# Branch merging in the list of weight blocks, gate blocks of the third mixer in the second's heads, token rows by DMA, query norm in the output norm

## The reference

```
u = rmsnorm(h) * valid                          # h: 16 learned tokens, 512 tokens
a_*, b_*, c_*, gate_logits = split(u @ w_in)    # 3 x 1024 columns are gate logits
y_a = hgrn2(...)          # 4 heads, decays per channel
y_b = gated_deltanet(...) # 4 heads: q, k, v = silu(conv(.)); q, k = l2norm; q *= 128**-0.5
                          # log decay and beta: one value per token and head
y_c = gla(...)            # 4 heads of 64 channels, decays per channel
# each mixer: y = rmsnorm(o, w) * silu(g) per head
proj   = einsum('blne,ned->blnd', [y_a, y_b, y_c], w_branch)     # 3 x (512 -> 1024)
merged = sum(sigmoid(gate_logits) * proj, over the 3 branches)
h = h + merged @ w_out
h = h + hierarchical_moe(rmsnorm(h))            # top 1 of 4 groups, top 2 of its 8 experts
return rmsnorm(h)                               # of the 512 tokens
```

## Time and profile before

| | |
|---|---|
| median of three runs | 1236.06 us |
| the runs | 1233.9 to 1239.37 us |
| the profiled execution | 1235.11 us |
| its span | 1233.3 us |
| granted clock of TensorE, mean | 0.944 |
| PE busy | 1083.6 us (88%) |
| PEld busy | 652.1 us (53%) |
| DVE busy | 466.2 us (38%) |
| ACT busy | 284.3 us (23%) |
| POOL busy | 57.1 us (5%) |

### The profile page before, as it was taken

The page is one execution under the profiler, slowest core; times in us unless marked ns, Lnnn a source line. Parts: engine busy times, 40 slices in busy tenths (PEclk is TensorE's granted clock), DMA queues, the critical chain, the costliest instruction groups (busy, mean ns, idle before and its releaser), DMA issues.

```text
span 1233.3 us, 15605 instructions
## 1 busy us (share of the span) xinstructions
PE 1083.6 (88%) x6346; PEld 652.1 (53%) x6346; DVE 466.2 (38%) x950; ACT 284.3 (23%) x540; POOL 57.1 (5%) x66
## 2 busy tenths in 40 slices
PE   6999999989989999899899898998974888788690
PEld 5665666665756757564645544443553444444350
DVE  3536354456373553734324321332335111111124
ACT  2524334133241332413203216000000111011012
POOL 0000000000000000000000000000001111111110
PEclk9999999999999999999999999998975998898995
DMA  9221222211111112112220105406331999999965
GB/s 282 63 69 52 68 52 69 52 52 35 38 49 35 52 36 52 35 35 56 64 53 26 52 26 210 131 0 236 127 120 35 413 415 408 401 396 402 417 231 219
DMA packets 113886, 171.53 MB, mean 139 GB/s; under 512 B 8726, under 2 KB 90855, under 8 KB 105507
## 3 DMA queue, kind: packets, MB, share of 16 engines
q1 hardware_dynamic: 100818, 131.19, 31.2%
q10 hardware_dynamic: 8080, 31.00, 6.6%
q0 software_dynamic: 4928, 8.50, 2.0%
HBM read 166.47 MB, written 12.58 MB: 145 GB/s over the span
## 4 chain that ended last, share of the span: by engine, by line
PE 73%; DMA 11%; DVE 9%; ACT 3%; issue 2%; POOL 1%; SPq 0%; POOLq 0%; DVEq 0%; ACTq 0%
PE ps L669 22%; DMA gates<-normed_tokens,gates 10%; PE ps L666 7%; PE ps L667 7%; PE ps L1583 7%; PE ps L1609 5%; PE ps L1910 4%; DVE arena L1197 3%; PE ps L1903 2%; PE ps L714 2%; PE ps L1897 2%; PE ps L723 2%; PE ps L693 1%; POOL expert_results L1871 1%; DVE yT L2189 1%
## 5 line engine op out<-in xcount | busy, mean ns | idle before, releaser
L669 PE MATMUL ps<-arena 128*128 128x512 f32 x672 | 317.5, 609 | 1.6 <-ACT arena L1162 1.6
L669 PEld LDWEIGHTS ps<-arena 128*128 128x128 f32 x672 | 120.9, 192 | 119.5 <-issue 114.3
L666 PE MATMUL ps<-arena 128*128 128x264 f32 x416 | 129.4, 393 | 10.0 <-DVE arena L1197 8.7
L667 PE MATMUL ps<-arena 128*128 128x264 f32 x416 | 128.1, 390 | 0.0
L1903 PE MATMUL ps<-arena,gates 128*64 128x256 f32 x1024 | 118.3, 385 | 1.5 <-DVE gates L2017 1.5
L1197 DVE TENSOR_TENSOR arena<-arena 128x512 f32<-128x512 f32 (+6 forms) x186 | 86.7, 511 | 83.9 <-ACT arena L1024 67.1
L1903 PEld LDWEIGHTS ps<-arena,gates 128*64 128x64 f32 x1024 | 74.7, 140 | 55.8 <-issue 23.5
L666 PEld LDWEIGHTS ps<-arena 128*128 128x128 f32 x416 | 75.7, 193 | 24.7 <-issue 14.9
L667 PEld LDWEIGHTS ps<-arena 128*128 128x128 f32 x416 | 80.1, 193 | 13.9
L1583 PE MATMUL ps<-yT,arena 128*128 128x512 f32 x192 | 84.4, 603 | 2.8 <-DVEq L93 2.8
L1910 PE MATMUL ps<-arena,gates 128*64 128x512 f32 x256 | 75.3, 719 | 0.0
(11 more groups left out here) (307 smaller groups left out, 1193.3 us busy)
## 6 DMA issues: line engine op xcount, KB each, us to landing
arena<-in_w_in SPq DMA_DIRECT2D x68, 512.0 KB, 3.9
arena<-in_expert_w_gate SPq DMA_DIRECT2D x32, 1024.0 KB, 10.0
arena<-in_expert_w_up SPq DMA_DIRECT2D x32, 1024.0 KB, 13.0
arena<-in_expert_w_down ACTq DMA_DIRECT2D x28, 1024.0 KB, 12.1
arena<-in_w_branch SPq DMA_DIRECT2D x8, 768.0 KB, 4.8
arena<-in_w_out SPq DMA_DIRECT2D x1, 4096.0 KB, 12.9
arena<-in_expert_w_down SPq DMA_DIRECT2D x4, 1024.0 KB, 13.3
arena<-expert_results SPq DMA_DIRECT2D x8, 512.0 KB, 6.8
```

The costliest lines, as they stand in the source:

```text
L666: t.matmul(dst[:, 0:HALF], wt, uT[:, k, 0:HALF], start=(k == 0), stop=(k == KD - 1))
L667: mm = t.matmul(dst[:, HALF:], wt, uT[:, k, HALF:], start=(k == 0), stop=(k == KD - 1))
L669: mm = t.matmul(dst, wt, uT[:, k, META:], start=(k == 0), stop=(k == KD - 1))
```

## The change

1. **The merge joins the list.** Its 12 blocks stand behind the segments of c: ("m", "ab", n), n = 0 to 7, is the a and b part of output column n (8 steps), three of them in the first round of c, five in the second; ("m", "c", n), n = 0 to 3, is the c part of two columns (8 steps), all at the end of the list, two of its blocks for each group of four columns. Their weights take slots of the same ring. On DVE merged(n) multiplies both parts with their gates and adds, within the levels of c; merged_last(n) does the c part. The loop L1574 to L1583 goes.
2. **Gate blocks.** t0 to t3 of the two rounds of c move to the four heads of b, two to each, which now hold four. Fills in b change: six steps before the sum for k and four before the products of k and k, then fill(4) twice around the transposes, where it was two, and fill(2) instead of fill(1) ahead of a level's second product.
3. **Gates in the mixers.** The sigmoid is made of Abs, Exp and Ln on ACT (gate_begin), a minimum and a difference on DVE (gate_part), and Exp on ACT (gate_end), inside the mixers.
4. **Token rows by transfer.** In the third head of a PE transposes log decay sums and beta into 20 rows of 256, which go to HBM once. In each head of b two DMAs on POOL's queue bring them back, broadcast over the 128 partitions (128 x 5 x 128 each). The POOL copies and the products G and B go; DVE's pass that takes the difference reads SBUF.
5. **Query norm.** q is no longer normalised. The sum over o squared gets a second matmul over q squared, with the small constants in its bias, so that the factor of q falls out of the output norm. The sum for q, its logarithm, its inverse root and the product go.
6. **Gates g.** In b and c the raw g is copied to SBUF early (gc), and v's blocks wait for that copy instead of the product.

```diff
         A_SEGS = ["f", "q", "g", "v", "t0", "t1"]
...
-        C_SEGS = ["k", "q", "g0", "g1", "v0", "v1", "t0", "t1", "t2", "t3"]
-        blocks = ([("a", s, r) for r in range(A_R) for s in A_SEGS] + [("b", s, r) for r in range(B_R) for s in B_SEGS] +
-                  [("c", s, r) for r in range(C_R) for s in C_SEGS])
+        C_SEGS = ["k", "q", "g0", "g1", "v0", "v1"]
+        M_AT = [3, 5]
+        blocks = [("a", s, r) for r in range(A_R) for s in A_SEGS]
+        for r in range(B_R):
+            blocks += [("b", s, r) for s in B_SEGS] + [("c", f"t{2 * (r % 2) + n}", r // 2) for n in range(2)]
+        n_first = 0
+        for r in range(C_R):
+            blocks += [("c", s, r) for s in C_SEGS] + [("m", "ab", n) for n in range(n_first, n_first + M_AT[r])]
+            n_first += M_AT[r]
+        blocks += [("m", "c", n) for n in range(4)]
...
         def mixers_gpsimd(g):
-            g.wait_ge(*dve0.after("gkm"))
+            g.wait_ge(*dve0.after("gbrow"))
+            g.dma_start(rows_dram, token_rows).then_inc(sem("rows_sent"), 16)
+            g.wait_ge(sem("rows_sent"), 16)
+            rv = rows_dram.rearrange("(t h) (k p) -> k h t p", h=B_R, k=2)
             for r in range(B_R):
                 g.wait_ge(*(b_pe.after(f"o.{r - 1}") if r else a_dve.after(f"y.{A_R - 1}")))
-                g.tensor_copy(t5(b_la), head_col(q_la, r)).then_inc(*b_pool.did(f"la.{r}"))
-                g.tensor_copy(t5(b_be), head_col(q_beta, r)).then_inc(*b_pool.did(f"be.{r}"))
+                g.dma_start(t5(b_gr), rv[0, r].unsqueeze(0).broadcast_to([P, NTP, P])).then_inc(sem("decay_rows"), 16)
+                g.dma_start(t5(b_br), rv[1, r].unsqueeze(0).broadcast_to([P, NTP, P])).then_inc(sem("beta_rows"), 16)
...
+                    if seg[0] == "t":
+                        t.wait_ge(*gate_read("b", int(seg[1]) % 2, 2 * r + int(seg[1]) // 2))
+                    elif seg == "k":
+                        if r:
+                            t.wait_ge(*m_dve.after(f"ab{2 * ((M_AT[0] - 1) // 2)}"))
+                        else:
+                            t.wait_ge(*gate_read(*channel_gates(B_R - 1, 0)))
+                    else:
+                        t.wait_ge(*c_dve.after({"q": "k", "g0": "f", "g1": "q", "v0": "gc_0", "v1": "gc_1"}[seg] + f".{r}"))
+                elif seg == "ab":
+                    if r == 0:
+                        t.wait_ge(*b_dve.after(f"y.{B_R - 1}"))
+                    if r in (0, 1, M_AT[0], M_AT[0] + 1):
+                        t.wait_ge(*c_act.after(f"vc_{1 - r % 2}.{int(r >= M_AT[0])}"))
+                    else:
+                        t.wait_ge(*m_dve.after(f"ab{r - 2}"))
+                elif r == 0:
+                    t.wait_ge(*m_dve.after(f"ab{KD - 1}"))
                 else:
-                    t.wait_ge(*c_dve.after({"q": "k", "g0": "f", "g1": "q", "v0": "g_0", "v1": "g_1"}[seg] + f".{r}"))
+                    t.wait_ge(*c_dve.after(f"y_{CH - 1}.{C_R - 1}"))
...
+                if stage == "m":
+                    if seg == "ab":
+                        b, wt, rhs = (k // 4, r), ring[:, n % RING, k, :], yT[:, k, :]
+                        first, last = k % 4 == 0, k % 4 == 3
+                    else:
+                        b, wt, rhs = (2, r // 2 * 4 + k % 4), ring[:, n % RING, k, :], yT[:, KD + r % 2 * 2 + k // 4, :]
+                        first, last = r % 2 == 0 and k < 4, r % 2 == 1 and k >= 4
+                    mm = t.matmul(merge_bank[b], wt, rhs, start=first, stop=last)
+                    if k == KD - 1:
+                        mm.then_inc(sem("block_done"), 1)
...
-                sums(bank(4), b_d[:, 0:SEQ]).then_inc(*b_pe.did(f"ss.{r}"))
+                t.matmul(bank(4), ones[:, :], b_d[:, 0:SEQ], start=True, stop=False)
+                t.matmul(bank(4), ones[:, :], b_kb[:, 0:SEQ], start=False, stop=True).then_inc(*b_pe.did(f"ss.{r}"))
...
                 through("b", "q", r)
-                t.wait_ge(*b_pool.after(f"la.{r}"))
-                t.wait_ge(*(b_dve.after(f"y1.{r - 1}") if r else a_dve.after(f"y1.{A_R - 1}")))
-                for c in range(NTP):
-                    mm = t.matmul(pair(6)[:, c * P:(c + 1) * P], b_la[:, c * P:(c + 1) * P], inc, start=True, stop=True)
-                mm.then_inc(*b_pe.did(f"G.{r}"))
-                fill(3)
+                fill(6)
                 t.wait_ge(*b_act.after(f"kk.{r}"))
                 t.wait_ge(*(b_act.after(f"ri.{r - 1}") if r else a_act.after(f"ri.{A_R - 1}")))
                 sums(pair(4)[:, 0:512], b_kb[:, 0:512])
                 sums(pair(4)[:, 512:], b_kb[:, 512:]).then_inc(*b_pe.did(f"ssk.{r}"))
-                fill(3)
-                t.wait_ge(*b_pool.after(f"be.{r}"))
-                t.wait_ge(*b_dve.after(f"dif.{r}"))
-                t.wait_ge(*b_act.after(f"eg.{r}"))
-                for c in range(NTP):
-                    mm = t.matmul(pair(6)[:, c * P:(c + 1) * P], b_be[:, c * P:(c + 1) * P], ident, start=True, stop=True)
-                mm.then_inc(*b_pe.did(f"B.{r}"))
                 through("b", "v", r)
+                fill(4)
                 t.wait_ge(*b_dve.after(f"kb.{r}"))
                 products(pair(4), b_kf, b_kb).then_inc(*b_pe.did(f"KK.{r}"))
-                fill(4)
-                t.wait_ge(*b_act.after(f"qq.{r}"))
-                sums(pair(6)[:, 0:512], b_vn[:, 0:512])
-                sums(pair(6)[:, 512:], b_vn[:, 512:]).then_inc(*b_pe.did(f"ssq.{r}"))
                 through("b", "g", r)
                 t.wait_ge(*b_dve.after(f"U.{r}"))
                 turn(pair(4), b_u).then_inc(*b_pe.did(f"N.{r}"))
-                t.wait_ge(*b_act.after(f"lnq.{r}"))
+                t.wait_ge(*(b_dve.after(f"y1.{r - 1}") if r else a_dve.after(f"y1.{A_R - 1}")))
                 turn(pair(6), b_kf).then_inc(*b_pe.did(f"kT.{r}"))
...
+                fill(4)
+                t.wait_ge(*b_dve.after(f"qr.{r}"))
                 t.wait_ge(*b_act.after(f"N.{r}"))
                 gram(bank(4), b_kf[:, P:], b_qf[:, P:]).then_inc(*b_pe.did(f"QK.{r}"))
-                fill(2)
...
-                    fill(1)
+                    fill(2)
...
-                    fill(1)
+                    fill(2)
...
-            assert not left
             c_out(C_R - 1)
+            fill(4)
             c_sum(C_R - 1)
+            fill(len(left))
         def mixers_scalar(a):
-            def gate(stage, n, r):
+            def gate_begin(stage, n, r):
+                g, row = gate_no(stage, n, r), gates[:, gate_row(stage, n, r), :]
                 a.wait_ge(*block_done(stage, f"t{n}", r))
-                a.activation(gates[:, gate_blocks.index((stage, f"t{n}", r)), :], real(n % 2), ACT.Copy).then_inc(sem("gate_read"), 1)
+                a.activation(row, real(n % 2), ACT.Abs).then_inc(sem("gate_size"), 1)
+                a.wait_ge(sem("gate_size"), g)
+                a.activation(row, row, ACT.Exp, scale=-1.0).then_inc(sem("gate_small"), 1)
+                a.wait_ge(sem("gate_small"), g)
+                a.activation(row, row, ACT.Ln, bias=one_c).then_inc(sem("gate_soft"), 1)
+            def gate_end(stage, n, r):
+                row = gates[:, gate_row(stage, n, r), :]
+                a.wait_ge(*gate_read(stage, n, r))
+                a.activation(row, row, ACT.Exp).then_inc(sem("gate_made"), 1)
...
                     tt(c_dve, f"y_{s}.{r}", yT[:, 8 + 2 * r + s, :], c_zz[s], c_g[s])
+            def gate_part(stage, n, r):
+                row = gates[:, gate_row(stage, n, r), :]
+                v.wait_ge(sem("gate_soft"), gate_no(stage, n, r))
+                v.scalar_tensor_tensor(row, real(n % 2), 0.0, row, ALU.min, ALU.subtract).then_inc(sem("gate_read"), 1)
+            def merged(n):
+                two = gates[:, n:2 * KD:KD, :]
+                if n == 0:
+                    v.wait_ge(sem("gate_made"), NB * KD)
+                v.wait_ge(*block_done("m", "ab", n))
+                v.tensor_tensor(two, ps[:, 2 * (n % 2) * 512:2 * (n % 2) * 512 + 1024].rearrange("p (b t) -> p b t", b=2), two, ALU.mult
+                                ).then_inc(*m_dve.did(f"ab{n}"))
+                v.wait_ge(*m_dve.after(f"ab{n}"))
+                tt(m_dve, f"s{n}", two[:, 0, :], two[:, 0, :], two[:, 1, :], ALU.add)
+            def merged_last(n):
+                row, sum_ = gates[:, 2 * KD + n, :], gates[:, n, :]
+                v.wait_ge(*block_done("m", "c", n // 4 * 2 + 1))
+                tt(m_dve, f"c{n}", row, merge_bank[2, n], row)
+                v.wait_ge(*m_dve.after(f"c{n}"))
+                tt(m_dve, f"h{n}", sum_, sum_, row, ALU.add)
...
+                        v.tensor_copy(c_g[l], real(1 - l)).then_inc(*c_dve.did(f"gc_{l}.{r}"))
+                    if l in (2, 3):
+                        s = l - 2
...
                             pick(c_dve, f"P{l - 1}_{s}.{r}", c_pm[s], l - 1, gram_bank(s))
+                    if l >= 4:
+                        merged(l - 4 + (M_AT[0] if r else 0))
                 for s in range(CH):
```

(12 more changed lines are left out.)

235 lines of the change are left out of this document (116 added, 119 removed).

## The result

| | before | changed |
|---|---|---|
| median | 1235.05 us (4 runs, 1233.9 to 1239.37) | 1216.62 us (4 runs, 1213.94 to 1217.12) |
| profiled execution, its span | 1235.11, 1233.3 us | 1213.94, 1212.1 us |
| ratio | | 0.9836, 95% interval 0.9816 to 0.9856 |

The change saves 18 us between the medians, 20 us by the ratio, 1.6%. Forecast were 1212 and a range of 1200 to 1226.

The account below looks back on a forecast made before the run. PE's work and waits were taken to bound the kernel. Terms +0.3 + 39.5 - 8.5 - 5 - 49.5 = -23.2 us on the profiled 1235.1 gave 1212 us, with an 8-in-10 range of 1200 to 1226.

Parts of the forecast that it names:

- What bounds it: Whole kernel to 751 us: time falls only by work taken from PE or waits filled; gain near 50 us, not 84.
- First mixer, +0.3: First mixer: extra gate passes cost nothing as PE never waits; transposed token rows add 0.3 us.
- Second mixer, heads 2 to 4, +9.7 each: Second mixer, per head: 11.3 us more PE work, 3.2 of waits gone, 1.6 of new wait at v's convolution.
- Second mixer, first head, +10.4: Second mixer's first head: the usual 9.7 us plus about 0.7 for token rows landing 5.5 us after issue.
- Third mixer, -8.5 and -5: Third mixer's two heads: v-block waits of 4.4 us go, first head has one block less; wait before level 5 stays.
- The end, -49.5: Last head's sums to output projection: 92.8 us becomes 43.3, with 27.5 of c blocks and 6.0 of idle PE.
- The remark that I left alone: Output projection: its first 32 products take 30.4 us where 27.5 would do; noted, with no term in the sum.
- More is hidden: Rival: v's convolution not late and clock stays up in the third mixer, giving 1202 us; chance 0.13.
- Less is hidden: Rival: second mixer keeps its waits and adds the new one, 12.9 us a head, giving 1225; chance 0.16.
- Rows late: Rival: second-mixer token rows land late; each us over 11.5 costs 4, slower than before from 17.5; chance 0.05.
- the port that the prediction named beside this rival: Token-row transfers from GpSimd: stall while VectorE holds the shared SBUF port, adding below 1 us, no change of the sum.
- Hold-up among merges: Rival: DVE merge passes awaiting PE blocks delay level work; eight at 3 us each leave no gain, near 1236; chance 0.06.

Follow-up runs that it names:

- the repeat: The changed kernel itself, unedited, run again on the same chip as three of the edits: 1218.56 us, ratio to before 0.9872.
- the split kernel: Changed kernel with the output projection started after four of the eight merged columns are summed, the rest after the last sum: 1209.89 us.
- the kernel with four edits: Changed kernel with first head's rows sent early, third-mixer state passes and gate copy behind the picks, and projection split: 1191.58 us, ratio 0.964.
- the one with five edits: Changed kernel with first rows early, states and gate copy behind picks, projection split, and v's convolution first: 1182.53 us, ratio 0.9579.

## Why the prediction was right, and where it was off

**What bounds it.** Right. PE's work and waits explain each stretch, and the gain is work removed and waits filled, not the 84 us of the merge. Of the 13.9 us less of PE's busy time, some 9.6 are the small products that went (2.2 and 0.2 in each of four heads) and a part of the rest is the clock, which reads 0.50 in four places between 250 us and the end of the merge products where it did in five. So filling is only a part of the 20 us. What it is worth in the rounds shows in the run with the blocks behind them: the gain falls from 18 to 20 us to 3 to 5.

**First mixer, +0.3.** -0.7. The first y of the kernel is already 0.9 earlier, so this lies in the setup, which the change hardly touches, and I count it as scatter: the first y comes between 95.7 and 96.7 us in these traces. The term itself is there: the way from the second to the third y, with the transposed rows in it, is 53.0 us in each kernel that has them and 52.8 in the two that have not.

**Second mixer, heads 2 to 4, +9.7 each.** Measured +9.6. The three waits at the sum of k, vT and the first level went; the new one at v's convolution came, 1.8 where I had 1.4 to 1.6. The edit that puts the convolution first took 1.7 back in each head, so its cause is shown. The parts' prices hold one by one: query norm -0.2 a head (-0.2 foretold), rows by transfer -3.0 (-2.2 of work, and the wait that I let go anyway). The rule that PE notices late rows 1.4 us after DVE nearly held: 1.7, from DVE's wait of 8.1 and PE's of 6.4.

**Second mixer, first head, +10.4.** Measured +13.6, the term that was mis-sized and the most of the error in the sum. The step was the landing time: I took 5.5 us from rows of other transfers that spread from 3.9 to 9.5. In this head the decay rows come 8.0 us after their issue (256.08 to 264.09), and in the run with late rows 7.8 (348.79 to 356.60). The nearest row by queue and kind was POOL's direct transfer, 7.2, and I should have stayed with it. POOL also issues 0.5 us behind the end of y, where I had it at once. That the late rows cost this head its excess is shown by the edit that sends for them early: the head then takes 8.5 to 10.1 more than before, around the 9.7 of the others. In the trace the head's 13.6 are 12.7 of PE's work time (86.8 against 74.0) and 0.8 of waiting (7.2 against 6.4). I had 11.3 of work, and 0.9 less waiting. Of the 12.7, 11.0 are what the other heads gain too, and 1.7 are a second fall of the clock (0.96 over this head where it was 0.98), for which the sum had no term. The waits are 1.7 longer than I had them. The one before the sum for k, which I let shrink by 1.0, went from 2.3 to 2.0 only, since the rows are late. The one at the v block, to which PE now comes earlier because G's products are gone, grew from 1.3 to 2.9, and I had nothing for it; moving the rows does not touch it. In the repeat PE waits 3.8 before the sum for k, not 2.0, and there no fall of the clock stands between the v block and that wait; that a slower PE hides a part of the lateness is my reading of these two traces and wasn't tested.

The estimate by the Trainium skill, page "DMA: Bandwidth & Descriptors", section "Anatomy of one DMA", about 2 us and bytes at 436 GB/s, was 2.8 us. The traces disagree: for these transfers of 640 pieces of 512 bytes, two in a row, it took 7.0 to 8.0 us from issue to landing for the first of each pair in the changed kernel, and 8.2 is the median of all eight. The measurement decides.

**Third mixer, -8.5 and -5.** Measured -8.6 and -5.3, and the nearness of both is partly luck, since errors cancel. In the first round I added 0.9 for the second matmul of the output sum, which the four heads of the second mixer had already been charged with, one each; PE's work fell by 6.9 (87.5 to 80.6), one block, and not by 6.0. Against that the wait at level 1 is 1.8 and not 1.1, so the waits fell by 1.8 and not by 2.5. In the second round the waits fell by 3.4 where I had 4.1, for the same reason, and PE's work time by 1.9 for the same work where I had 0.9: one fall of the clock less (0.98 where it was 0.96). The 3.0 before level 5 stayed, as said.

**The end, -49.5.** Measured -49.9. 27.7 us of c blocks for 27.5, 5.5 of idle PE for 6.0, 1.4 for 1.3. The remark that I left alone, 30.4 where 27.5 would do, was worth 2.2 us in the changed kernel, where the granted clock reads 0.50 until 822.7.

**The rivals.** *More is hidden*: no. *Less is hidden*: no, each head keeps one wait. *Rows late*: the mechanism is real and its side too, since with rows that come 16.8 us behind a head's output products in heads 2 to 4 (9.0 later and 7.8 of landing) the kernel is 0.45% slower than before, where the sum, with late rows in all four heads, had it 0.2% faster and the border at 17.5. In the change itself the decay rows of these heads land 7.0 to 7.4 us after their issue, and DVE wants them 9.7 after it (339.88 to 349.56), so it ran some 2.5 us from a wait of DVE. Whether the port that the prediction named beside this rival slows such a transfer, no run here tests. *Hold-up among merges*: 0.8 us at a k block, 1.4 ahead of the c blocks, and 0.8 at a merge block where a gate block had waited as long before; no more.

**The sum.** -23.2 foretold, -21.2 measured in the span. The first head cost 3.2 more than foretold. All other stretches together came out 1.2 lower, 1.0 of it in the first mixer's scatter, and that was luck. The profiled execution lies 2.7 below the median of its four runs, which puts the median at 1216.6, 4.6 above the forecast.

## What to carry to other kernels

Moving a long tail product into a list of filler work is worth only the waits that it covers and the falls of the clock that go with them, not its own length: count the waits before, here 4 us in a head of the second mixer and 9 to 12 in a round of the third. Where no transfer was involved, the price of each stretch then followed within a few tenths, in part because errors cancelled. After such a change look for what DVE does in which order at each wait that is left: three waits (1.8 in each head, 3.0 and 1.8 in each round) were passes that nobody wanted yet, standing ahead of the one that PE wanted, and moving them brought about 20 us, as much as the whole change. An idle stretch of PE costs more than its length when the clock falls behind it: a wait of 3.0 cost 4.7 in all, one of 5.5 cost 7.6.

## What the runs showed of the hardware

The granted clock behind an idle stretch isn't the same from run to run, for the same program in the same place. PE idles 3.0 us before level 5 in each round of the third mixer; the second round of the changed kernel, then both rounds of the kernel with the split projection (its edit is behind these rounds), then the first round with the convolution of v first:

```profile
695.44:781.89 86.45, 79.86 (x467) 0.98 0.07 25
```

```profile
607.64:697.23 89.59, 81.93 (x485) 0.96 0.20 53
697.23:785.17 87.94, 81.34 (x467) 0.96 0.07 25
```

```profile
599.75:686.38 86.63, 78.97 (x485) 1.00 0.20 55
```

The same products take 79.0 to 81.9 us of PE in a first round. Six kernels have the wait of 3.0 there: behind it the clock cost nothing in one (79.0), about 1.7 us in four (80.6), and 3 us in one (81.9). The loss doesn't need so long a wait: in the second round of the split kernel (702.7 to 706.0 us) and in the same round of the kernel with four edits (691 to 694 us) the granted clock reads 0.50 behind a wait of 1.8. In that last kernel the round reads 0.98 and takes 81.6 us, though the waits before levels 1 and 5 are gone; the same round takes 79.9 us at 1.00, with the same wait of 1.8, in the kernel with only the states and the copy moved and in the one with five edits. A good part of the scatter of this kernel, 5 to 10 us between runs, can come from such places, at 1.7 us each: that is an estimate from these rounds and wasn't measured by itself. The spread of four runs doesn't sort by the waits that are left: 2.4 us for the kernel with five edits, 1.8 for the one with the state passes moved alone.
